# Two norms per layer: a first pair of groups on activations without the norm's factor, a second pair with the contraction outermost

## The reference, cut to what matters

```python
def rms_norm(x, g):
    xf = x.astype(F32)
    y = xf * lax.rsqrt(jnp.mean(xf * xf, axis=-1, keepdims=True) + NORM_EPS)
    return (y * g.astype(F32)).astype(x.dtype)
...
        u = rms_norm(h, norm_mix_g[layer])
        p = u @ w_in[layer]
...
        h = h + merged @ w_o[layer]
        u = rms_norm(h, norm_ffn_g[layer])
        h = h + conv_glu(u, w_up[layer], conv_w[layer], conv_b[layer], w_down[layer])
    return rms_norm(h, norm_final_g)
```

## Time and profile before

| | us |
|---|---|
| median of 3 runs | 2047.35 (2044.59 to 2056.27) |
| the profiled execution | 2048.42, of which 2046.5 are the span of the profile |
| PE busy | 1883.6 (92%) |
| DVE, ACT, POOL busy | 1293.0 (63%), 1140.5 (56%), 1037.9 (51%) |
| mean granted TensorE clock | 0.959 |
| DMA | 271.20 MB, mean 133 GB/s |

### The profile page before, as it was taken

How to read it: one execution, slowest core, us unless ns; L and a number is a source line. 1 busy time by engine, 2 the same in 40 slices (tenths; PEclk the granted TensorE clock), 3 DMA queues, 4 the chain that set the end, 5 groups by cost and what they waited for, 6 DMA issues and landing times.

```text
span 2046.5 us, 44566 instructions
## 1 busy us (share of the span) xinstructions
PE 1883.6 (92%) x16390; PEld 1778.9 (87%) x16390; DVE 1293.0 (63%) x1943; ACT 1140.5 (56%) x1924; POOL 1037.9 (51%) x742
## 2 busy tenths in 40 slices
PE   8889889999999889888999999988899998879999
PEld 8778779999999778778999989866899997669999
DVE  3487725669913397824669963476786536777764
ACT  5653455456755654445557755665555457465544
POOL 5663449839986573448929985741200045411000
PEclk9999989999999999979999999997999999779999
DMA  6432015656665432005656664420366653205665
GB/s 208 122 103 71 23 39 158 176 145 186 188 187 164 124 114 74 23 22 154 176 151 179 187 173 133 150 89 21 112 183 202 193 166 113 72 17 154 186 193 173
DMA packets 146922, 271.20 MB, mean 133 GB/s; under 512 B 16433, under 2 KB 16946, under 8 KB 146738
## 3 DMA queue, kind: packets, MB, share of 16 engines
q1 hardware_dynamic: 145296, 264.97, 45.2%
q10 hardware_dynamic: 1442, 3.66, 0.5%
HBM read 267.52 MB, written 1.05 MB: 131 GB/s over the span
## 4 chain that ended last, share of the span: by engine, by line
PE 65%; DVE 15%; ACT 9%; POOL 8%; issue 3%; DMA 0%; ACTq 0%; DVEq 0%; SPq 0%
PE bank L649 63%; POOL ring_split L1317 8%; ACT arena L1351 7%; ACT hi_ring L1351 1%; PE bank L758 1%; DVE arena L1891 1%; DVE u L1961 1%; DVE arena L1890 1%; DVE arena L2062 1%; DVE arena L1975 1%; DVE arena L1974 0%; DVE arena L2109 0%; DVE arena L1973 0%; ACT L1351 0%; DVE arena L2464 0%
## 5 line engine op out<-in xcount | busy, mean ns | idle before, releaser
L1317 POOL TENSOR_TENSOR ring_split<-ring,hi_ring 128x512 fp32r<-128x512 f32 x682 | 969.1, 1449 | 736.7 <-ACT hi_ring L1351 730.9
L1351 ACT ACTIVATE hi_ring<-ring 128x512 fp32r<-128x512 f32 x1002 | 619.3, 630 | 555.1 <-PE bank L649 532.0
L649 PE MATMUL bank<-u_hi,hi_ring 128*128 128x256 f32 (+1 forms) x2480 | 676.1, 285 | 47.3 <-POOL ring_split L1317 39.7
L649 PE MATMUL bank<-u_split,hi_ring 128*128 128x256 f32 (+1 forms) x2480 | 665.4, 281 | 1.6 <-DVE u_split L1966 1.4
L649 PE MATMUL bank<-u_hi,ring_split 128*128 128x256 f32 (+1 forms) x2480 | 665.0, 281 | 0.0
L649 PEld LDWEIGHTS bank<-u_hi,hi_ring 128*128 128x128 f32 (+1 forms) x2480 | 452.3, 188 | 61.8 <-POOL ring_split L1317 41.1
L649 PEld LDWEIGHTS bank<-u_split,hi_ring 128*128 128x128 f32 (+1 forms) x2480 | 452.4, 188 | 4.0 <-DVE u_split L1966 2.4
L649 PEld LDWEIGHTS bank<-u_hi,ring_split 128*128 128x128 f32 (+1 forms) x2480 | 452.2, 188 | 0.9
L1999 DVE TENSOR_TENSOR ring_split<-ring,hi_ring 128x512 fp32r<-128x512 f32 x320 | 215.3, 694 | 111.9 <-ACT hi_ring L1351 108.1
L649 PE MATMUL bank<-arena 64*64 64x64 f32 (+6 forms) x3680 | 240.3, 255 | 14.6 <-DVE arena L2109 9.3
L649 PEld LDWEIGHTS bank<-arena 64*64 64x64 f32 (+3 forms) x3680 | 210.4, 155 | 49.5 <-issue 29.7
(11 more groups left out here) (246 smaller groups left out, 2407.0 us busy)
## 6 DMA issues: line engine op xcount, KB each, us to landing
ring<-in_stream SPq DMA_DIRECT2D x1002, 256.0 KB, 2.8
par<-in_params ACTq DMA_DIRECT2D x3, 637.0 KB, 4.3
h<-in_x SPq DMA_DIRECT2D x4, 256.0 KB, 4.3
cst<-in_cst SPq DMA_DIRECT2D x1, 993.0 KB
out<-h ACTq DMA_DIRECT2D x3, 256.0 KB, 2.8
par<-in_params ACTq DMA_DIRECT2D x1, 633.0 KB, 8.3
out<-h ACTq DMA_DIRECT2D x2, 128.0 KB, 2.3
msk<-in_masks SPq DMA_DIRECT2D x1, 104.0 KB
```

The costliest lines, as they stand in the source:

```text
L649: ins = nc.tensor.matmul(o, l, r, start=start, stop=stop)
L1317: G.tensor_tensor(ring_lo[:, c, :], ring[:, c, :], hi_ring[:, q % HI_RING, :].bitcast(F32), ALU.subtract).then_inc(lo_by_pool, 1)
L1351: return nc.scalar.activation(o, i, f, **kw)
```

## The change

Ahead of each norm, ACT now also writes `u_hi` = h * g (L1351 by `raw_high`) and DVE `u_lo` = h * g - u_hi (`raw_low`), part by part behind each addition to `h`, with no norm factor. TensorE multiplies the first two groups by these (`project_raw`), with the sums of squares as two ones-matmuls between its second and third feature tile; the 8 constant multiplications are gone. DVE writes the factor into the two banks (`rescale`), or, for cq0 and ckv and for U0 and U1 of the second kind, takes it in while it empties them. `u` is written when the raw pass has used a feature tile; the last part waits for the end of the raw pass. The next two groups (A2 and A3, U2 and U3, or cq1, kpe and aq) run with the feature tile outermost, over four output tiles in one run of 8 pieces, and end together. Their weights are stored in that order. For layer kind 2's first entry the gains of both norms are multiplied once (`gains`).

```diff
+                def project_across(place, enter, leave=False, beside=None, with_ones=0):
...
+                    q = W.take(names[0], 4 * KD)
+                    for n in names[1:]:
+                        W.ends[n] = W.ends[names[0]]
...
                     for k in range(KD):
                         for w, a in ((0, 0), (1, 0), (0, 1)):
+                            enter(k, w, a)
+                            for t, (n, o) in enumerate(place):
...
+                        if beside:
+                            beside(k)
...
-                norm_total("norm2", squares, 0)
-                project_first(("U0", "U1"), 5, 8)
-                for i in range(2, 22):
+                project_raw(("U0", "U1"), past, lambda k: norm_total("norm2", squares, "sums_ready", past["sums_ready"] + 1) if k == 1 else None)
+                project_normed([("U2", 0), ("U2", T), ("U3", 0), ("U3", T)], 5)
+                for i in range(4, 22):
```

ACT:

```diff
-            def last_squares(C, dst, names, fresh, last=False):
+            def raw_high(C, gain, part_):
+                for k in range(part_.start, part_.stop):
+                    ins = A(u_hi[:, k, :], h[:, k, :], ACT.Copy, scale=gain[:, k:k + 1])
+                C.link(ins, S["raw_hi"])
+
+            def last_squares(C, dst, names, fresh, gain, params_ready, last=False):
+                act.wait_ge(params_in, params_ready)
                 for j, (name, part_) in enumerate(zip(names, PARTS)):
                     hi.upto(name, HI_RING if j < 3 else LEAD)
                     act.wait_ge(S["h_ready"], past["h_ready"] + fresh + j + 1)
                     C.link(A(dst[:, part_, :], h[:, part_, :], ACT.Square), S["squares_ready"])
...
+                    raw_high(C, gain, part_)
...
-                    if j > 1:
-                        hi.make(at + HI_RING + j - 1)
+                    hi.make(at + HI_RING + j + 4)
...
+                hi.upto(LAST_WO[-1], HI_RING + 2)
                 guess_norm(C, B, "norm2", "ffn")
-                hi.upto(LAST_WO[-1], HI_RING)
+                hi.upto(LAST_WO[-1], HI_RING + 3)
...
                         hi.upto(f"U{i}")
                         bank = B.wait(act, f"U{i}")
+                        if i < 2:
+                            act.wait_ge(S["raw_scaled"], past["raw_scaled"] + 2 + i + 1)
```

DVE:

```diff
+                    if j in (1, 2, 4):
                         dve.wait_ge(S["squares_ready"], past["squares_ready"] + 5 * which + j + 1)
+                        add_squares(C, dst, min(j, 3), S["sums_ready"])
...
+                    raw_low(C, gain, part_, 5 * which + j + 1)
...
+                        if j < n - 1:
+                            dve.wait_ge(S["raw_used"], past["raw_used"] + first // 5 * 4 + j + 1)
+                        else:
+                            B.wait(dve, raw_last)
...
-                    if j > 2:
-                        lo.make(at + HI_RING + j - 2)
+                    lo.make(at + HI_RING + j + 3)
+
+            def rescale(C, B, names):
+                for name in names:
+                    bank = B.wait(dve, name)
+                    C.link(V.tensor_tensor(v3(bank[:, :], 2), v3(bank[:, :], 2), spread(rn[:], 2), ALU.mult), S["raw_scaled"])
...
+                    if i < 2:
+                        bank = B.wait(dve, f"U{i}")
+                        C.link(V.scalar_tensor_tensor(hidden[:, 2 * i:2 * i + 2, :], v3(bank[:, :], 2), 0.0, spread(rn[:], 2), ALU.max, ALU.mult))
+                        B.release(dve, f"U{i}")
+                    else:
+                        dve.wait_ge(S["conv_in"], past["conv_in"] + 4 + i - 1)
```

More of the change, by code:

```diff
@@ L347, in groups1 @@
 def groups1(last=False):
[L348 removed]
+    g = ["A0", "A1", "norm"] + [f"A{i}" for i in range(2, 7)] + ["Bq0", "Wup0", "Aup0", "Wup1", "Aup1", "Gup0", "Gup1", "Bq1"]
     g += ["KK0", "KK1", "Bf0", "Bf1", "Cq0", "Cq1", "BON0", "BON1", "Ck"]
@@ L368, in groups1, with groups2 @@
         g += [m2[0] for m2 in MERGE[i + 1:i + 2]] + [m[1]]
-    g += [*LAST_WO, "norm2"] + [f"U{i}" for i in range(22)] + ["D0"] + ["positions"] * last + [*LAST_D[1:], "norm"] + ["gained"] * last
+    g += [*LAST_WO, "U0", "U1", "norm2"] + [f"U{i}" for i in range(2, 22)] + ["D0"] + ["positions"] * last + [*LAST_D[1:]]
     return g
[L373 to L378, removed]
+def groups2(first=False):
+    g = ["cq0", "ckv", "norm"] + ["gained"] * first + ["cq1", "kpe", "aq", "ak", "ncq", "nckv", "av", "nq", "nk", "qk0", "qk1"]
     g += ["uq0", "uq1", "uk0", "uk1", "uv", "rq", "rk", "nlq0", "nlq1", "nlk0", "nlk1", "if", "mv0", "mv1"]
@@ L389, in groups2 @@
     g += ["bn", "ln", "mn0", "mn1"]
-    g += [*LAST_WO, "norm2"] + [f"U{i}" for i in range(16)] + [*LAST_D, "norm"]
+    g += [*LAST_WO, "U0", "U1", "norm2"] + [f"U{i}" for i in range(2, 16)] + [*LAST_D]
     return g
@@ L1710, in _ @@
                 last = l + 1 == layers[0]
-                last_squares(C, next_squares, LAST_D, 5, last)
-                guess_norm(C, B, "norm", "next")
-                hi.upto(LAST_D[-1], HI_RING)
+                last_squares(C, next_squares, LAST_D, 5, gains if last else PAR1.of(par, "g_mix"), (stage + 1) * 16, last)
+                hi.upto(LAST_D[-1], HI_RING + 2)
+                guess_norm(C, stage_banks[stage + 1], "norm", "next")
+                hi.upto(LAST_D[-1], HI_RING + 3)
                 if last:
@@ L1933, in add_last @@
                     bank = B.wait(dve, name)
+                    if j == 0 and gain is not None:
+                        dve.wait_ge(params_in, params_ready)
+                    if last and j == 0:
+                        C.link(V.tensor_tensor(gains, PAR2.of(par, "g_final"), PAR2.of(par, "g_mix"), ALU.mult))
                     o = h[:, part_, :].rearrange("p a t -> p (a t)")
@@ L1950, in final_scale, with norm_parts @@
                     C.link(ins)
-            def norm_parts(C, gain, buf, first, at, scale=None):
+            def norm_parts(C, B, raw_last, gain, buf, first, at, scale=None):
                 n = len(HEAD_PARTS)
```

232 lines of the change are left out of this document (122 added, 110 removed).

## The result

The changed kernel takes **2107.16 us** (2097.91 to 2116.55, 4 runs), the kernel before on the same chip 2049.32 (2044.59 to 2056.27): a ratio of **1.028** (95% interval 1.022 to 1.034), slower by some 58 us. I had forecast slower by 16, in a range up to 2075. The direction came true; the size did not.

A forecast was written before the change was run, and what follows sets the result against it. Entries bound by the norm's chain and by how far ACT and DVE have prepared pieces. Mixing entries -8.5, FFN entries +3.0 and +11.2, parameters +10.4: +16.1 on 2048.42, less 1.1 for the median, 2063 us; range 2036 to 2075.

The forecast's parts named there:

- the clock: At stalls of 3.9 us and more (entries 2, 4, 6, 8, first D): 1.7 us each for the lower clock.
- What goes: From T, the end of the last output matmul: the raw pass fills the gap, 6.3 us at entries 2, 3, 4, 7.
- First kind, piece 12: Entries 1 to 4: piece 12, cast behind both raw banks, stalls TensorE at least 2.3 us (mixing) or 3.9 (FFN).
- the collisions: Pieces 8 to 11: POOL's casts block DVE's writes of u, some three times, up to 0.9 us each.
- the middle: First kind: piece 12 taken midway between 9.5 and 12.2 us (FFN), 7.9 and 10.2 (mixing) after the raw pass.
- the upper end: First kind: with collisions piece 12 comes up to 12.2 us (FFN) or 10 (mixing) after the raw pass.
- Second kind, mixing: Entries 5 and 7: for piece 12 only POOL's collisions count; shorter by 2.5 us each.
- Second kind, FFN: Entries 6 and 8: DVE's queue makes piece 12 late, a stall of 4.6 us; +3.9 each, +5.6 with the clock.
- Parameters: Starts of D: ACT's casts queue behind the wait for load_params; +8.7 us, +10.4 with one clock drop more.
- The rival that the table load hides the wait: Starts of D: the parameter wait hides under the table load, 2053 us; within the span of the 0.33 rival.
- every cover holds: All entries: preparation never binds, whole gaps (54.6 us) are gained, parameters cost 8.7: 2001 us; chance 0.12 with halfway forms.
- only the lower ends: No collisions, no clock drop: 2045 us, up to 2057 if the clock falls in the second kind alone; chance 0.33.

The follow-up runs named there:

- e8: Changed kernel with the parameters' wait behind D0's square, pieces 12 to 15 ahead, angles behind D1's part, DVE writing remainders of pieces 8 to 11: 1.0079.
- e2: Changed kernel, but ACT or DVE prepares pieces 12 to 15 ahead of and between the two raw banks: 1.0125 of the kernel before.
- e1: Changed kernel, but ACT waits for the layer's parameters behind the square of D0's part: 1.0197 of the kernel before.
- e10: Changed kernel with e1, e2 and e3, and the angles of the last first-kind layer ahead of D0's part: 1.0020 of the kernel before.
- e3: Changed kernel, but DVE instead of POOL writes the remainders of pieces 8 to 11 in six entries: 1.0201 of the kernel before.
- e14: e10 with four constant multiplications ahead of the wait for probabilities, before transpositions in the attention stretches: 0.9992 of the kernel before.
- e15: Kernel before the change with only the constant multiplications ahead of the attention's transpositions added: 0.9983 of the kernel before.

## Why the prediction was wrong in size

Two terms of its sum were too small: the waiting behind the raw pass in the first kind (step 2 below, some 7 us in the profiled run) and the clock (step 7), and two things had no term: the output tail of the first kind and the angles (step 6). By its own steps:

1. **What goes** was right: TensorE runs on at T, and the raw pass takes 12.7 us at entry 2 (429.54 to 442.23 in e8's trace, and as long in the changed kernel's), for which I had 12.65.
2. **First kind, piece 12: the step that failed.** The mechanism came as written, a wait ended by POOL 144 matmuls into the entry; the size of the waiting was wrong. TensorE waits at pieces 9 and 11 (0.8 to 1.3 us each, the collisions) and then still 3.6 (mixing) and 4.35 (FFN) at piece 12. Together that is 6.1 and 5.7 us at entries 1 and 3, where I had 2.3 to 4.4 and took 3.4, and 6.8 at entries 2 and 4, where I had 3.9 to 6.6 and took 5.6 (the 30.8 I took is a little above the middle, 30.5). So the middle was wrong, and the upper end, which the measured 1.77 us spoke for, was still too small in mixing. That the order of the queues makes piece 12 late, e2 shows: 34 us went locally without taking any work away. The four entries together missed **17.7 us of the 46** in the profiled run (+5.6 twice for +1.5, +4.3 and +1.7 for -1.5 and -2.0). Of these some 7 are this waiting, 2 the output tail, which had no term (TensorE waits 1.07 and 0.85 us for DVE at the FFN entries; I had counted DVE's added work in the tail in the second kind only), and 3 to 4 the clock of step 7; the rest, some 5, I cannot assign.
3. **Second kind, mixing:** entry 7 was right (-2.1 for -2.5). Entry 5 gained nothing: TensorE's waits there are 2.82, 1.30, 1.79 and 1.61 us, 7.5 in sum, where I had 2.4 and 2.7. These 2.4 us more match the 2.6 missed.
4. **Second kind, FFN:** right in the number, in part by luck. The wait at piece 12 was 4.37 us, ended by DVE (forecast 4.6), the entries +7.0 and +6.9 for +5.6. But the listed work adds up to 7.7 + 0.9 + 3.5 + 2.9 + 4.2 + 5.2 + 0.7 = T + 25.1 for piece 12's remainder, not the T + 28.2 that I wrote, and so to a stall of 1.7. At entry 6 the trace has the root starting at T + 8.4, this remainder at T + 26.6 and TensorE wanting it at T + 22.4: both were earlier than I had, by 1.6 and 1.0, and the difference came out. The clock took 3.7 and 1.8 us of TensorE's busy time more than before, where I had 1.7 each.
5. **Parameters:** nearly right. TensorE waits 3.7, 3.6 and 2.1 us more at the three starts of D, 9.4 for the 8.7 forecast, and e1 removed 11.7 locally, for 10.4 with the clock. The rival that the table load hides the wait fell: ACT stood 2.63 us for `par`.
6. **Angles, no term.** I had named DVE's extra work at the boundary only behind the sums. But the same queue holds the angles behind D0's part: with 3 us of rest before and ACT's added copies, raw parts and blocked operations in front, the rest was used up, ACT's casts queued behind the wait for `h`, and TensorE waited 6.13 for 2.86. With the clock that is most of the 7.6 missed in that D.
7. **The clock, the second failing step.** I counted 1.7 us per stall in five places, 8.5. By the span times one less its mean granted clock the changed kernel lost 125 us at half clock, before 84. Of these 41, 28 lie at the entries and in D, mostly 1.7 to 5.1 us per place. Not all of that is time lost, since TensorE is waiting for part of it: counted over its busy time alone it is some 19 us, for the 8.5. The other 13 lie in mixing stretches that the change does not touch and in part come and go with the run (-4.3 for +4.2 in layer 2). The mean clock of all runs, 0.946 for 0.958, says that some of the loss is always there: 0.012 of 2107 is 25 us, nearly half of it. These microseconds are counted within the stretches of steps 2 to 6 too and do not add to them.
8. **D itself** ran slower at full clock, by 3.2 us in the last one and some 2 in the one before, not forecast and not explained.

The rivals: "every cover holds" fell with piece 12, and "only the lower ends" with the collisions. Once the orders are mended (e10), time times clock is 1961 us for the 1965 of before: by that measure the whole change, with all that e10 adds, saves 4 us and not the 54.6 of the rival. Other waits stand behind the gap: entry 2 of e10 is only 1.4 us shorter than before, with waits of 1.07 us in the tail and of 0.3 to 0.8 at six pieces.

## What to carry to other kernels

When a gap at a join is filled, ask first how far each engine has prepared when it turns to the results of what now fills it; a look-ahead tied to the ends of groups shrinks when groups begin to end together. Put preparation between such tasks, not behind them, and put a wait for data directly ahead of its first use, with nothing queued behind it. Price a wait on TensorE by the clock as well: here the stretches with a wait of over 4 us lost a further 2.3 to 3.7 us of TensorE's busy time to the half clock in the profiled run.

## What the runs showed of the hardware

**Two pitches of the same products.** In the last D, 579 matmuls of identical shape took 65.3 us in the kernel before and 67.9 in the changed kernel at a granted clock of 1.00 in both, with no wait in between: 1.360 or 1.413 us for each piece.

```profile
1970.50:2035.80 65.30, 65.30 (x579) 65.30 (x578) 35.36 (x53) 30.34 (x48) 0.00 (x0) 1.00 0.66 193
```

```profile
2030.20:2098.10 67.90, 67.90 (x579) 67.90 (x578) 35.37 (x52) 30.36 (x49) 0.00 (x0) 1.00 0.64 186
```

The changed kernel showed 1.413 there twice, and so did all other variants but e2, e3 and e14, which had 1.360, and e15, which had both within this D. It is not the program alone: in the first D the same changed kernel ran 291 matmuls in 34 us in one run (606 to 640) and 302 in the other (604 to 638), both at clock 1.00 and without a wait, and that is the 1.9 us between the table's two columns there. Nothing here tells what sets it.

**Blocking in pairs.** Two DVE products of SBUF operands beside POOL's casts took 2.81 us for 0.87 (1.77 in the earlier trace rows). DVE's products of the raw banks, which have one operand in PSUM, took 1.43 us for two beside a cast of POOL in the changed kernel (459.53 beside 459.44) and 1.42 in e3 with POOL idle: not held up. The Trainium skill (SBUF — State Buffer, section "SBUF: two separate sides") says that GpSimd and a DVE instruction with two SBUF inputs take the shared port in turn, each for its whole instruction; both figures agree with it.
